# Moving five weight-residual subtractions from VectorE to GpSimd, and selection rounds into the stick-breaking stage

## The reference

```
proj = rmsnorm(h) @ w_in
group A: indexer scores I[t,s] = sum_h w[t,h] relu(q_idx . k_idx); each query keeps its top-k keys; softmax attention over them
group B: stick-breaking attention, A[t,s] = exp(z_ts + sum_{s<=j<t} logsigmoid(-z_tj))
group C: means over trailing windows 2/4/8/16, minus x, then a per-group linear map
h += concat(A, B, C) @ w_out
h += ConvFFN(rmsnorm(h));  h += sigmoid(rmsnorm(h) @ w_ple_gate) * (p @ w_ple_proj)
```

## Time and profile before

| | us |
|---|---|
| median of 3 runs | 1719.51 |
| lowest, highest | 1717.09, 1720.02 |
| profiled execution, device time | 1722.34 |
| its span, first to last instruction | 1720.5 |
| TensorE busy | 1637.9 (95%) |
| VectorE busy | 885.7 (51%) |
| ScalarE busy | 681.6 (40%) |
| GpSimd busy | 271.3 (16%) |

### The profile page before, as it was taken

How to read it: one execution, slowest core, us unless ns; L and a number is a source line. 1 busy time by engine, 2 the same in 40 slices (tenths; PEclk the granted TensorE clock), 3 DMA queues, 4 the chain that set the end, 5 groups by cost and what they waited for, 6 DMA issues and landing times.

```text
span 1720.5 us, 31176 instructions
## 1 busy us (share of the span) xinstructions
PE 1637.9 (95%) x12030; PEld 1487.6 (86%) x12032; DVE 885.7 (51%) x1567; ACT 681.6 (40%) x981; POOL 271.3 (16%) x448
## 2 busy tenths in 40 slices
PE   5999979999999999998999999799999999999898
PEld 4787836799999999997978786369999999999898
DVE  5657884144555553322748488632355555522325
ACT  3344544235444442224443344532444444322241
POOL 2320240021111111000104105101111111100000
PEclk9999989699999999998999999888999999999989
DMA  5133142132223232332322311322232322233321
GB/s 163 51 95 81 32 134 74 30 86 74 85 85 98 79 89 80 89 92 75 86 75 79 103 48 55 94 66 69 72 89 85 94 85 85 80 92 89 98 61 57
DMA packets 225670, 140.07 MB, mean 81 GB/s; under 512 B 13074, under 2 KB 219684, under 8 KB 225504
## 3 DMA queue, kind: packets, MB, share of 16 engines
q1 hardware_dynamic: 223172, 133.32, 26.9%
q0 software_dynamic: 2400, 5.42, 1.0%
HBM read 131.06 MB, written 7.65 MB: 81 GB/s over the span
## 4 chain that ended last, share of the span: by engine, by line
PE 83%; DVE 10%; ACT 2%; issue 2%; DMA 1%; POOL 0%; DVEq 0%; SPq 0%; POOLq 0%; ACTq 0%
PE ps L1624 24%; PE ps L1626 23%; PE ps L1625 23%; DVE score L1285 2%; DVE m L1282 2%; PE ps L1930 1%; PE ps L2005 1%; PE ps L1687 1%; DVE w_L L1184 1%; PE ps L1773 1%; PE ps L1917 1%; PE ps L1873 1%; PE ps L1927 1%; DVE stat L1403 1%; PE ps L1651 1%
## 5 line engine op out<-in xcount | busy, mean ns | idle before, releaser
L1184 DVE TENSOR_TENSOR w_L<-w_raw,w_H 128x1024 fp32r<-128x1024 f32 (+4 forms) x236 | 257.3, 1099 | 443.7 <-ACT w_H L822 443.7
L1624 PE MATMUL ps<-bH,w_H 128*128 128x272 f32 x1664 | 481.9, 290 | 1.4 <-ACT projT L822 1.4
L1626 PE MATMUL ps<-bH,w_L 128*128 128x272 f32 x1664 | 480.2, 289 | 0.0
L1625 PE MATMUL ps<-bL,w_H 128*128 128x272 f32 x1664 | 478.5, 288 | 0.0
L822 ACT ACTIVATE w_H<-w_raw 128x1024 fp32r<-128x1024 f32 (+4 forms) x236 | 220.0, 943 | 298.6 <-PE ps L1626 298.3
L1624 PEld LDWEIGHTS ps<-bH,w_H 128*128 128x128 f32 x1664 | 313.5, 188 | 2.3 <-ACT projT L822 1.9
L1625 PEld LDWEIGHTS ps<-bL,w_H 128*128 128x128 f32 x1664 | 314.5, 189 | 0.2
L1626 PEld LDWEIGHTS ps<-bH,w_L 128*128 128x128 f32 x1664 | 313.4, 188 | 0.0
L1624 PE MATMUL ps<-actH,w_H 128*128 128x272 f32 x704 | 204.1, 290 | 0.0
L1626 PE MATMUL ps<-actH,w_L 128*128 128x272 f32 x704 | 203.7, 289 | 0.0
L1625 PE MATMUL ps<-actL,w_H 128*128 128x272 f32 x704 | 202.7, 288 | 0.0
(11 more groups left out here) (318 smaller groups left out, 2427.2 us busy)
## 6 DMA issues: line engine op xcount, KB each, us to landing
w_raw<-in_w_up SPq DMA_DIRECT2D x88, 512.0 KB, 3.8
w_raw<-in_w_down SPq DMA_DIRECT2D x32, 512.0 KB, 3.6
w_raw<-in_w_in SPq DMA_DIRECT2D x24, 512.0 KB, 4.9
w_raw<-in_w_ple_gate SPq DMA_DIRECT2D x16, 512.0 KB, 3.7
w_raw<-in_w_down SPq DMA_DIRECT2D x16, 384.0 KB, 3.2
w_raw<-in_w_out SPq DMA_DIRECT2D x16, 320.0 KB, 3.4
w_raw<-in_w_in SPq DMA_DIRECT2D x8, 452.0 KB, 3.5
w_raw<-in_w_in SPq DMA_DIRECT2D x8, 384.0 KB, 3.2
```

Of the source, the lines that this page charges most:

```text
L1184: ins = dve.tensor_tensor(w_L[u % SPLIT][:, a:b], w_raw[raw_slot(l, u)][:, a:b], w_H[u % SPLIT][:, a:b].bitcast(F32), ALU.subtract)
L1624: pe.matmul(out, wh, xh, start=start, stop=False)
L1625: pe.matmul(out, wh, xl, start=False, stop=False)
L1626: return pe.matmul(out, wl, xh, start=False, stop=stop)
```

## The change

GpSimd gets a `split` of its own, which subtracts over the whole 128 x 1024 unit, and does units 17, 18 and 19 before `pool_means(0)` and units 20 and 21 after it, before the stores of b_k. It waits for the high half and for `w_lo` of the units before. VectorE's five splits go. The rounds are cut differently: 3 more of them (of block 3, 512 columns) lie before the end of the stick-breaking stage, and the softmax stage has 2 in place of 5; one more round of block 1 stands before `stick_max(0)`. `decode_queries` moves from u = 6 to u = 3. The arithmetic is the same.

```diff
--- before.py
+++ after.py
@@ -696,6 +696,18 @@
                 pool.memset(qim, 0.0)
                 pool.memset(qbm[:], 0.0)
 
+                def split(u):
+
+                    pool.wait_ge(w_hi, at(w_hi, u + 1))
+                    pool.wait_ge(w_lo, at(w_lo, RAW + u))
+                    hold(pool)
+                    pool.tensor_tensor(w_L[u % SPLIT][:, :], w_raw[raw_slot(l, u)][:, :], w_H[u % SPLIT][:, :].bitcast(F32),
+                                       ALU.subtract).then_inc(w_lo, 1)
+
+                split(17)
+                split(18)
+                split(19)
+
                 def pool_means(m):
@@ -738,6 +750,9 @@
                 pool_means(0)
+                pool.wait_ge(pooled_ok, at(pooled_ok, 1))
+                split(20)
+                split(21)
                 for t in range(TILES):
@@ -1360,29 +1375,24 @@
-                select(1, 2, 7)
+                select(1, 2, 8)
                 stick_max(0)
                 stick_max(1)
                 feature_out(3)
-                split(17)
-                select(1, 7, 16)
-                select(2, 0, 4)
+                select(1, 8, 16)
+                select(2, 0, 5)
                 feature_out(4)
-                split(18)
-                select(2, 4, 7)
+                select(2, 5, 9)
                 stick_max(2)
                 stick_max(3)
                 feature_out(5)
-                split(19)
-                select(2, 7, 16)
-                select(3, 0, 2)
+                select(2, 9, 16)
+                select(3, 0, 4)
                 feature_out(6)
-                split(20)
-                select(3, 2, 5)
+                select(3, 4, 8)
                 stick_max(4)
                 stick_max(5)
                 feature_out(7)
-                split(21)
                 dve.wait_ge(u_ev, at(u_ev, 2))
@@ -1391,7 +1401,7 @@
-                select(3, 5, 11)
+                select(3, 8, 14)
@@ -1454,9 +1464,9 @@
                     a_norm(u)
                     if u + 2 < 12:
                         row_max(u + 2)
-                    if u < 5:
-                        select(3, 11 + u, 12 + u)
-                    elif u == 6:
+                    if u < 2:
+                        select(3, 14 + u, 15 + u)
+                    elif u == 3:
                         decode_queries()
```

## The result

The changed kernel takes 1725.8 us (median of 9 runs, 1722.1 to 1728.4) against 1719.4 us for the kernel before on the same chip (9 runs, 1717.1 to 1723.7): a ratio of 1.0033, with a 95% interval of 1.0023 to 1.0043. The medians differ by 6.4 us, and the interval of the ratio covers a loss of 4.0 to 7.4 us. Its profiled execution has a span of 1724.0 us and a time of 1725.76 us.

A forecast was written before the change was run, and what follows sets the result against it. TensorE (95% busy) and VectorE were taken to arrive together in the stick stage, VectorE's order of work to bind the softmax stage. Layers' +2.8 and +3.6 us give +6.4 on the 1719.51 median: 1725.9 us, range 1719.5 to 1730.

The forecast's parts named there:

- part 1: Stick-breaking stage: five splits leave VectorE (5.65 us per layer), take 2.06 us each on GpSimd, and cost the end nothing.
- The rule against the change: Shared SBUF ports: a VectorE subtraction meeting a GpSimd split waits up to 2.06 us, swallowed by the later stall.
- part 2: Stick-breaking stage, three more rounds: the one before stick_max(0) starts remainders(0) 1.2 us later.
- The stage ends 0.3 us later: End of the stick-breaking stage, layer 1: row_max(0) starts at 226.0 in place of 225.7.
- part 3: GpSimd's later marks: all 1.2 us later, with d_zero at 244.45 in layer 1.
- part 4: Softmax stage: VectorE waits 5.6 us for d_zero before decode_queries; turns of u = 7 +2.8 and +3.6 us, together +6.4.
- The clock: TensorE behind the softmax stall: low clock for a_logits(7), 1.65 us of matmuls; full clock for a_logits(8), 0.92 us.
- The clock stays high: Rival, softmax stall: turns and a_logits(7) run at full clock, +1.5 and +2.3 us, 1723.3 us; chance 0.17.
- The clock comes back late: Rival, behind the softmax stall: a_logits(8) is slow too, +0.85 us a layer, 1727.6 us; chance 0.08.
- stick_max(0) has hidden slack: Rival, stick-breaking stage: the extra round costs no 1.2 us, total +4.0 us, 1723.5 us; chance 0.08.
- Later waits swallow it: Rival, after the softmax stall: later waits absorb half or more, within 3.4 us, about 1720.5 us; chance 0.12.
- decode_queries does not wait: Rival, softmax stage: qam is cleared before 238.9, turns of u = 7 3 us early per layer, 1713.5 us; chance 0.07.

The follow-up runs named there:

- experiments 1: Changed kernel with the decode_queries call put back at u = 6, nothing else: 1718.2 us, ratio 0.9991.
- experiment 5: Kernel before with only decode_queries moved from u = 6 to u = 3: 1731.4 us, ratio 1.0065.
- experiment 8: Changed kernel with GpSimd's splits of units 20 and 21 moved to the decode stage, beside MAX8 and MATCH_REPLACE: 1728.9 us, ratio 1.0059.
- 11: Changed kernel with decode_queries back at u = 6 and splits 20 and 21 in the decode stage, extra round kept: 1713.3 us, ratio 0.9962.
- experiment 2: Changed kernel with the extra round back behind stick_max(0), measured twice: 1726.9 us (ratio 1.0046) and 1725.4 us (1.0027).
- 7: Kernel before with only the one extra round put ahead of stick_max(0): 1720.5 us, ratio 1.0006.
- 10: Changed kernel with decode_queries back at u = 6 and the extra round back behind stick_max(0): 1718.4 us, ratio 0.9987.
- 9: Changed kernel with decode_queries at u = 6, extra round back behind stick_max(0), splits 20 and 21 in the decode stage: 1713.4 us, ratio 0.9967.

## Why the prediction was right, point by point

Predicted 1725.9 us, measured 1725.8; the loss predicted at 6.4 us, measured at 6.4. The cause is the early call of decode_queries with the stall and the slow matmuls behind it, by experiments 1 and 5. That the numbers meet to 0.1 us is luck: the interval reaches from 4.0 to 7.4 us, and the stage says 6.0. And terms on the way were wrong, which did not show because the moment at which qam is cleared sets the time of what follows.

- **Splits on GpSimd (part 1).** Estimated 2.06 us, measured 2.35 to 2.36, and 2.56 and 2.60 for the late two: the split takes 2.3 ns for a column where the add took 2.0, and no run shows why. The page "GPSIMD Engine Reference" of the Trainium skill, section "3.1 Elementwise — side-by-side cycle accounting", gives about 2.6 cycles per element for two inputs; at the 1.2 GHz that it uses, an estimate of 2.2 us for 1024 columns, which is nearer to the 2.35 of the trace. They ended at 219.1 where I had 218.3, and the store behind them still had 2.35 us to wait for ScalarE. So the price on the end was nothing, as predicted.
- **The rule against the change.** The port rule was true here: the pair of subtractions went from 1.31 to 3.49 us, +2.2 where the prediction allowed up to 2.06. The prediction said that the stall would swallow it. It did: without the hold (experiment 8) the changed kernel is no faster. But the sum for the stage's end left it out, and once the stall is gone it is not swallowed (experiments 1 and 11).
- **The extra round (part 2).** TensorE idle for 1.2 us before remainders(0): 1.16. Right, in both layers. What it costs in the end is open (below).
- **"The stage ends 0.3 us later": wrong.** Row_max(0) was predicted at 226.0 and came at 228.51. Experiment 8 splits the error: with the subtraction free, row_max(0) comes 93.2 us after the first MAX8, in the changed kernel 95.4, before 92.5. So 2.2 us are the port and 0.7 the rounds and the gap, where the sum had 0.3.
- **d_zero (part 3).** Predicted 244.45, measured 243.81 + 0.74 = 244.55. Right; in layer 2 1086.08 + 1.2 = 1087.28 followed from it, and it was 1086.83 + 0.74 = 1087.57.
- **The stall (part 4).** VectorE was to wait 5.6 us and waited 2.62: it came later by the 2.5 us of the point before, and by about half a us that I did not follow up. Its end was right, and only the end counts. With the subtraction free (experiment 8) the wait is 5.05 us, close to the 5.6, but 0.9 of it is a later qam. The prediction also had TensorE standing for 5 us, and "as long" as VectorE in its list of signs: it stood 2.59 us in layer 1 and 4.34 in layer 2. It was to be done with a_logits(6) at 243 and was at 245.5. Both signs missed by half in layer 1, and the errors cancel since both engines go on from the same moment, the cleared qam.
- **The clock.** The low level for a_logits(7), 1.65 us, and the high one for a_logits(8), 0.92 us, were as predicted, but not for the reason given. The prediction took the clock as hardly risen when the stall began; it was back at 1.00 by 246 and fell again at 248.5, when the stall had ended. That it came back before a_logits(8) was one of several outcomes: it did not in experiments 5 and 8 and in the second profile of experiment 2. Turns of u = 7: predicted 257.6 and +3.6 us in layer 2, measured 257.19 and 1100.13 - 1096.85 = +3.3. As differences, 2.4 and 3.3 us against the 2.8 and 3.6 predicted.
- **The rivals.** "The clock stays high" is excluded by the rows at 248.79 and 249 to 251. "The clock comes back late" did not happen in the profiled execution, but in the second one of experiment 2 and in experiments 5 and 8. "stick_max(0) has hidden slack" is excluded by the gap of 1.16 us. "Later waits swallow it" and "decode_queries does not wait" did not happen: the turns of the later steps keep the distance (257.14 and 259.79 us at u = 8).

**What stays open.** The extra round costs 1.2 us up to a_logits(0) in every trace, and 2.2 to 3.1 us for both layers together up to the turns of u = 7 in three comparisons (before with 7, 10 with 1, 9 with 11). Yet the same comparisons give +1.0, +0.7 and -0.8 us by the ratios, and the two measurements of experiment 2 against the changed kernel -2.2 and +1.1; each is uncertain by about 2 us, and their mean is zero. So these runs cannot tell the price of the round from nothing. The stretch between the layers, which moves by over 5 us from one execution to the next with its share of low clock, is enough to hide it, and so is the scatter of a_out(3) within it, 2.80 us in some layers and 4.4 to 5.4 in others; no run shows that the round is given back there. Nor was the move of three rounds out of the softmax stage run by itself: that it brings time is argued from experiments 9 and 11, which have it together with the splits. And why the clock fell for 3.4 us behind one stall and for 10 behind another is not shown.

## What to carry to other kernels

Before an instruction is moved ahead in one engine's order, find when the other engines' signals that it waits for arrive: one clearing on GpSimd made a kernel that would have been level with the old one 0.3% slower, and the line cost 7 us. Lay work given to GpSimd beside VectorE instructions that it was not seen to hold up (here MAX8 and MATCH_REPLACE), not beside those that it did (here subtractions with two inputs, copies and scalar multiplications); the same two splits cost 3.5 to 5 us at the end of the stick stage and nothing that shows beside MAX8. While a stall set the time here, a gain ahead of it showed nothing or less than nothing: take the stall away first, then measure the rest. And a difference of 1 to 2 us is not read from two single profiled executions of such a kernel, nor from medians of a few.

## What the runs showed of the hardware

- While GpSimd subtracts (2.34 to 2.60 us), VectorE's subtraction pair grew from 1.31 to 3.49 us, its copies from 0.36 to 2.42, its scalar multiplications from 0.61 to 3.29 and even one of two columns from 0.17 to 1.49. MAX8 stayed at 0.46 and, at 512 columns, at 0.68. I had expected only the subtraction.
- Gaps of 2.6 and 4.3 us on TensorE (the changed kernel's two layers) each came with 3.4 us at a granted clock of 0.50 at their end or behind it, one of 6.2 us with 10 us of it (experiment 8), but one of 3.5 us also with 10 (experiment 5), and in the kernel of experiment 2 one of 3.7 us with 3.4 and one of 3.35 us with 6.8. So the price of a stall is not read from its length.
- Up to 8 us lay between single executions of one kernel. Two profiled ones (experiment 2) were 7.6 us apart, 6.3 of them outside the changed stage. The stretch between the two measured stages, with the same work on TensorE in every kernel, took 715.6 to 721.3 us, by and large the longer the more of it ran at the low level (41 to 55 us).
